# Another order of two stages of a two-block network on one core, and a gating multiply on GpSimd

## The chip, the cores and the metric

The kernel runs on one core of a Trainium2 chip, in float32 with split weights. The metric is the device time of one execution in microseconds (us). Before the change it is 1389.76 us, the median of 3 runs (1389.14 to 1390.28).

## The reference, cut to what matters

One sequence of 256 tokens, width 1024, goes through two layers and then a second block. Each layer is FFN, mixer, FFN. The mixer of layer 0 is causal attention (8 heads of 128, RoPE, normed q and k), that of layer 1 is a Mamba-2 mixer. What the change touches:

```python
# attention: o = softmax(q k^T) v per head, then
x = x + o @ w_o
# Mamba-2: 2048 inner channels, 8 groups of 4 heads of 64, state 128
proj = h @ w_in                      # z (2048), x B C (4096), dt (32)
xbc = silu(causal_conv4(xbc) + conv_b)
y = ssd_chunked(xs * dt, dt * a, B, C)   # two chunks of 128 tokens
y = (y + d_skip * xs) * silu(z)      # the gate
y = y * rsqrt(mean(y * y over each group of 256 channels) + eps) * norm_g
x = x + y @ w_out
```

## The kernel before

**Weights.** Every weight comes as a unit of 512 KB (4 k-tiles of 128 rows by 512 columns) into one of three slots of `raw`. ScalarE (ACT) copies it to `w_hi` in a reduced format (`split_hi`, L374 to L382), VectorE (DVE) subtracts to get `w_lo` (`split_lo`, L384 to L390), and TensorE (PE) multiplies three times, hi by hi, lo by hi, hi by lo. A unit's 24 matmuls of 512 columns set the pace. `split_hi` of unit n waits until PE has used unit n-3, the load of unit n until `w_lo` of unit n-3 is made. SyncE issues the loads.

**Order.** Each engine has one queue, in the order in which its function issues; semaphores join them. Nothing reorders at run time: whatever stands behind a waiting instruction waits too.

**Attention** (`attn_pe` L994, `attn_act` L1068, `attn_dve` L1152). Heads are worked off in slots (`head_slot_*`): in slot s head s is transposed, head s-1 gets its scores, head s-2 its probabilities transposed, head s-3 its output. From slot 5 on, PE fills in tiles of w_o from the table `fill`: `wo_tile(j, k)` is 6 matmuls of unit j with head k, and waits for `oT` of that head, which DVE makes (`prob_dve`, L1224) from ACT's `oT_hi`. In DVE's slot the bias (`bias_dve`, from the scores) comes first, then `oT_lo`, then the probabilities. Two splits of w_o, its units 2 and 3, are issued between slots: unit 2 ahead of slot 4's ACT work, unit 3 after slot 7's.

**Mamba stage** (`ssm_pe` L1283, `ssm_act` L1420, `ssm_pool` L1559, `ssm_dve` L1608). The x, B, C columns come in 8 chunks of 512 channels, channels on partitions: PE multiplies, ACT scales the first tap, DVE adds three taps per tile (12 steps a chunk, L1674), ACT applies Silu. PE turns the x chunks to rows (`ssm_turn`), and the B chunks too, into `b_rows`, which nothing reads. Then comes a loop over the 8 groups, j = 0 to 7, with two items (token chunks) each. PE: one unit of z (`z_unit`, two make a quarter of z), then `scores(2j)`, `scores(2j+1)`, then `outputs(2j-2)`, `outputs(2j-1)`. DVE: `differences` of the running sums, a `split_lo`, `finish` (adds the skip term, gives y), `weigh` (decay times scores). ACT: a copy of a quarter of z every other round (`copy_z` after the change), a split, `exps`, `cross_exps`, `silu_z`, and for a quarter of y `group_squares` and `group_scale`. GpSimd (POOL): `xdt` and `x_skip` of each item, `group_rstd`, and by DMA the running sums of two groups at a time into `cum_early` or `cum_late` (`load_cum`). DVE multiplies y by its gate (`gate_y`, L1714), a quarter at a time. PE then turns the scaled quarters (`turn_y`, L1381), ACT and DVE split them to `yT_hi` and `yT_lo`, and 8 units of w_out follow in the order `OUT_UNITS`: (column half h, quarter q) = (0,0), (0,1), (1,0), (1,1), (0,2), (0,3), (1,2), (1,3). All of the first four need the first two quarters.

Of the kernel before, what the change touches and what calls it, by code (L numbers as in the profile page):

```python
# [24 lines left out]
P = 128  # L25
SEQ = 256
# [118 lines left out]
def build(nc, w, out):  # L145
    with ExitStack() as ctx:
# [135 lines left out]
        b_rows = r("b_rows", [P, GROUPS, P])  # L282
# [711 lines left out]
        def attn_pe(pe):  # L994
            norm_pe(pe, 1, True)
            u = FIRST_UNIT["qkv"]
            for c in range(6):
                if c >= 2:
                    pe.wait_ge(sem("qkv_copied"), TT * (c - 1))
                for j in range(2):  # L1000
                    linear_unit(pe, u + 2 * c + j, 4 * j, KD, hT_hi, hT_lo, pair_banks(c),
                                ("hT", KD * 1) if c == 0 else None)
                    head_slot_pe(pe, 2 * c + j - FIRST_SLOT)
            pe.wait_ge(sem("qkv_copied"), TT * 6)
            u = FIRST_UNIT["wo"]

            def wo_tile(j, k):

                n = BY_ROWS[j][1]
                hi, lo = use_unit(pe, u + j)  # L1010
                pe.wait_ge(sem("oT"), k + 1)
                for t in range(TT):
                    to = psum[:, pair_banks(n)[t], :]
                    a, b = (o[:, k % 4, t * P:(t + 1) * P] for o in (oT_hi[k // 4], oT_lo[k // 4]))
                    pe.matmul(to, a, hi[:, k % 4, :], start=k == 0, stop=False)
                    pe.matmul(to, a, lo[:, k % 4, :], start=False, stop=False)
                    m = pe.matmul(to, b, hi[:, k % 4, :], start=False, stop=k == HEADS - 1)
                if k % 4 == 3:
                    m.then_inc(sem("unit_used"), 1)


            fill = {5: ((0, 0), (0, 1)), 6: ((1, 0), (0, 2)), 7: ((1, 1), (0, 3)), 8: ((1, 2), (1, 3)),
                    9: ((2, 4), (2, 5)), 10: ((2, 6), (3, 4)), 11: ((3, 5), (2, 7), (3, 6), (3, 7))}
# [44 lines left out]
        def attn_act(act):  # L1068
# [3 lines left out]
            for i in range(12):  # L1072
# [15 lines left out]
                split_hi(act, u + i + SLOTS)  # L1088
# [4 lines left out]
                head_slot_act(act, i - FIRST_SLOT)  # L1093
            u = FIRST_UNIT["wo"]
            for slot in range(12 - FIRST_SLOT, HEAD_SLOTS):
                head_slot_act(act, slot)
                if slot == 7:
                    split_hi(act, u + SLOTS)
# [53 lines left out]
        def attn_dve(dve):  # L1152
            u = FIRST_UNIT["qkv"]
            norm_dve(dve, 1, ("mix_norm", 0), True, second_and_third("qkv"))
            for i in range(12):
# [4 lines left out]
                split_lo(dve, u + i + SLOTS)  # L1160
# [3 lines left out]
                if i % 2 == 0 and 1 <= c <= ROPED:  # L1164
                    rope_dve(dve, c - 1)
            u = FIRST_UNIT["wo"]
            for slot in range(12 - FIRST_SLOT, HEAD_SLOTS):
                bias_dve(dve, slot)
                prob_dve(dve, slot)
                if slot == 7:  # L1170
# [96 lines left out]
        OUT_UNITS = [(h, 2 * pair + q) for pair in range(2) for h in range(2) for q in range(2)]  # L1267
# [15 lines left out]
        def ssm_pe(pe):  # L1283
# [22 lines left out]
            for c in range(CHUNKS):  # L1306
# [7 lines left out]
                if 1 <= c <= X_CHUNKS + B_CHUNKS:  # L1314
# [30 lines left out]
            def scores(i):  # L1345
# [4 lines left out]
                else:  # L1350
                    pe.wait_ge(sem("rows"), X_CHUNKS + B_CHUNKS)
# [32 lines left out]
            for j in range(ITEMS // 2 + 1):  # L1384
                if j < ITEMS // 2:
                    z_unit(j)
                    if j == 0:
                        pe.wait_ge(sem("a_sum"), 2)
                        pe.wait_ge(sem("head_rows"), 2)
                if j < ITEMS // 2:  # L1390
                    scores(2 * j)
                    scores(2 * j + 1)
                else:
                    turn_y(0)
# [3 lines left out]
            turn_y(1)  # L1398
            pe.wait_ge(sem("z"), 4)
            for i, (h, q) in enumerate(OUT_UNITS):  # L1400
                if i == 2:
                    pe.wait_ge(sem("y"), ITEMS)
                linear_unit(pe, FIRST_UNIT["ssm_out"] + i, 4 * q, KI, yT_hi, yT_lo, OUT_BANKS[h], ("yT", 0))
                if i in (1, 2):
                    turn_y(i + 1)

        def ssm_turn(pe, c):
# [4 lines left out]
            for i in range(4):  # L1412
                if c < X_CHUNKS:
                    for t in range(TT):
                        m = pe.transpose(psum[:, 4 + t, i * P:(i + 1) * P], xT[:, c % 2, i, t * P:(t + 1) * P], ident)
                else:
                    m = pe.transpose(psum[:, 4, i * P:(i + 1) * P], bcT[:, 4 * (c - X_CHUNKS) + i, 0:P], ident)
            m.then_inc(sem("rows_ready"), 1)

        def ssm_act(act):  # L1420
            norm_act(act, 4, ("mix_norm", KD), False, FIRST_UNIT["ssm_xbc"] - 1 + SLOTS)

            def copy_rows(c):
                act.wait_ge(sem("rows_ready"), c + 1)
                if c < X_CHUNKS:
                    act.activation(xs[:, :, 512 * c:512 * (c + 1)], psum[:, 4:6, :], ACT.Copy).then_inc(sem("rows"), 1)
                else:
                    g = 4 * (c - X_CHUNKS)
                    act.activation(b_rows[:, g:g + 4, :], psum[:, 4, :].rearrange("p (g n) -> p g n", g=4), ACT.Copy)\
                       .then_inc(sem("rows"), 1)  # L1430
# [13 lines left out]
            for c in range(CHUNKS):  # L1444
# [9 lines left out]
                split_hi(act, u + SLOTS)  # L1454
                if c == DT_CHUNK:
# [16 lines left out]
                split_hi(act, u + 1 + SLOTS)  # L1472
                if 1 <= c <= X_CHUNKS + B_CHUNKS:
                    copy_rows(c - 1)
                if c == CHUNKS - 1:
                    exps(0)
                    exps(1)
                    cross_exps(1)
                for i in range(4):
                    tile = 4 * c + i  # L1480
                    act.wait_ge(sem("conv_out"), tile + 1)
# [5 lines left out]
                if c == CHUNKS - 2:  # L1487
                    act.wait_ge(sem("a_sum"), 2)
                    cross_exps(0)
            def group_squares(q):  # L1490

                act.wait_ge(sem("y_gated"), q + 1)
# [25 lines left out]
            for j in range(ITEMS // 2 + 1):  # L1518
                q = j // 2
                if j < ITEMS // 2 and j % 2:  # L1520
                    act.wait_ge(sem("unit_used"), FIRST_UNIT["ssm_z"] + j + 1)
                    act.activation(z[:, :, 512 * q:512 * (q + 1)], psum[:, 0:TT, :], ACT.Copy).then_inc(sem("z"), 1)
                if j < ITEMS // 2:
                    split_hi(act, FIRST_UNIT["ssm_z"] + j + SLOTS)
                if j == ITEMS // 2:
                    act.wait_ge(sem("x_skip"), ITEMS)
                    turned_y(0)
                if 0 < j < ITEMS // 2:
                    exps(2 * j)
                    exps(2 * j + 1)  # L1530
                    if j < ITEMS // 2 - 1:
                        cross_exps(j + 1)
                if j in (3, 7):
                    silu_z(q - 1)
                    silu_z(q)
                if j in (5, 6):
                    group_squares(j - 5)
                if j == 7:
                    group_scale(0)
                    group_scale(1)  # L1540
            u = FIRST_UNIT["ssm_out"] + SLOTS
            turned_y(1)
# [16 lines left out]
        def ssm_pool(pool):  # L1559
# [23 lines left out]
            for i in range(ITEMS):  # L1583
# [16 lines left out]
                if i in (11, 13):  # L1600
                    group_rstd((i - 11) // 2)
# [6 lines left out]
        def ssm_dve(dve):  # L1608
# [5 lines left out]
            def differences(i):  # L1614
# [4 lines left out]
                for hh in range(HPG):  # L1619
# [3 lines left out]
                                             ALU.subtract, ALU.add).then_inc(sem("ssm_diff"), 1)  # L1623

            for c in range(CHUNKS):
# [40 lines left out]
                for j in range(2):  # L1666
                    dve.wait_ge(sem("conv_first"), 4 * c + 2 * j + 2)
# [12 lines left out]
                split_lo(dve, u + 1 + SLOTS)  # L1680

            def weigh(i):
                g, t = divmod(i, TT)
                dve.wait_ge(sem("decay"), i + 1)
                dve.wait_ge(sem("ssm_scores"), i + 1)
                over_heads = lambda scores: scores.unsqueeze(1).broadcast_to([P, HPG, P])
                dve.tensor_tensor(cum(i), cum(i), over_heads(psum[:, 4 + t, 0:P]), ALU.mult).then_inc(sem("within"), 1)
                if t == 0:
                    dve.wait_ge(sem("crossed"), HPG * (g + 1))
                    to = cross[:, g % 2, :, :]  # L1690
                    dve.tensor_tensor(to, to, over_heads(psum[:, 4, P:SEQ]), ALU.mult).then_inc(sem("within"), 1)
# [24 lines left out]
            for j in range(ITEMS // 2 + 1):  # L1716
                if 0 < j < ITEMS // 2:
                    differences(2 * j)
                    differences(2 * j + 1)
                    if j < ITEMS // 2 - 1:  # L1720
                        split_lo(dve, FIRST_UNIT["ssm_z"] + j + SLOTS)
                if j:
                    finish(2 * j - 2)
                    if j == ITEMS // 2:
                        dve.wait_ge(sem("ssm_out"), ITEMS)
                        lo_of_y(0)
                    finish(2 * j - 1)
                if j < ITEMS // 2:
                    weigh(2 * j)
                    weigh(2 * j + 1)  # L1730
                    if j == 0:
                        split_lo(dve, FIRST_UNIT["ssm_z"] + SLOTS)
                else:
                    split_lo(dve, FIRST_UNIT["ssm_z"] + j - 1 + SLOTS)
                if j in (4, 5):
                    gate_y(j - 4)
# [718 lines left out]
```

## Time and profile before

| | |
|---|---|
| median of 3 runs | 1389.76 us |
| profiled execution | 1387.17 us, its span 1385.4 us |
| PE busy | 1355.8 us, 98% of the span |
| DVE, ACT, POOL busy | 881.4, 710.5, 302.2 us |
| attention: heads and w_o | about 242 to 309 us of the span |
| Mamba stage: chunks; loop over groups; output | 707 to 791; 791 to 869; 869 to 915 us |

Busy time is the union of an engine's instructions. A row of the timeline gives start, length, engine, line, what it writes from what, the count of merged instructions, and in brackets how long the engine had stood and what released it.

### The profile page before, as it was taken

How to read it: one execution, taken by the hardware profiler on the slowest of the kernel's cores; microseconds unless marked ns; L12 is line 12 of the kernel's file. 1: busy time of each engine (PE TensorE's matmuls, PEld its weight loads, DVE VectorE, ACT ScalarE, POOL GpSimd, SP SyncE). 2: the span in 40 equal slices, each digit the busy share in tenths (PEclk: the TensorE clock that was granted, in tenths of full speed). 3: DMA queues.
4: the chain of work that ended last, by engine and by line, in shares of the span. 5: the costliest groups of instructions: out<-in, count | busy, mean ns of one | idle time of the engine just before them, and what ended most of it. 6: DMA issues, size and time to landing. Idle time of an engine off the chain costs nothing.

```text
span 1385.4 us, 19574 instructions
## 1 busy us (share of the span) xinstructions
PE 1355.8 (98%) x7607; PEld 1146.6 (83%) x7607; DVE 881.4 (64%) x912; ACT 710.5 (51%) x840; POOL 302.2 (22%) x230
## 2 busy tenths in 40 slices
PE   8999999999999999999999998999999999999997
PEld 7888888778888888888899976888888899888885
DVE  5445568746445565445578798566877556877576
ACT  6444455645444454444557678644434455557543
POOL 3300001000000000000000133029996001535740
PEclk9999999999999999999999999999999999999999
DMA  9555546526555555555454564489675544645341
GB/s 293 195 194 185 182 154 205 167 68 204 191 195 183 182 181 185 182 184 197 134 187 135 203 219 146 132 284 360 233 264 187 168 153 154 209 155 163 117 161 46
DMA packets 158286, 254.09 MB, mean 183 GB/s; under 512 B 8785, under 2 KB 99233, under 8 KB 156561
## 3 DMA queue, kind: packets, MB, share of 16 engines
q1 hardware_dynamic: 155136, 232.94, 51.3%
q0 software_dynamic: 2576, 18.45, 3.6%
q10 hardware_dynamic: 512, 1.85, 0.4%
q8 instruction: 43, 0.70, 0.2%
q14 instruction: 19, 0.15, 0.0%
HBM read 252.12 MB, written 1.08 MB: 183 GB/s over the span
## 4 chain that ended last, share of the span: by engine, by line
PE 81%; issue 8%; DVE 5%; ACT 3%; DMA 2%; SPq 0%; POOL 0%; ACTq 0%; POOLq 0%; DVEq 0%
PE psum L608 11%; PE psum L610 11%; PE psum L609 10%; PE psum L643 5%; PE psum L645 5%; PE psum L644 5%; PE psum L1796 4%; PE psum L1798 3%; PE psum L1797 3%; PE psum L428 3%; PE psum L430 3%; PE psum L429 3%; DVE w_lo L390 3%; ACT w_hi L382 2%; DMA raw<-in_ffn_w_up 1%
## 5 line engine op out<-in xcount | busy, mean ns | idle before, releaser
L390 DVE TENSOR_TENSOR w_lo<-raw,w_hi 128x2048 fp32r<-128x2048 f32 x220 | 548.7, 2498 | 334.0 <-ACT w_hi L382 333.6
L382 ACT ACTIVATE w_hi<-raw 128x2048 fp32r<-128x2048 f32 x220 | 421.3, 1916 | 347.6 <-PE psum L610 124.3
L608 PE MATMUL psum<-w_hi,hT_hi 128*128 128x512 f32 x704 | 278.7, 396 | 2.7 <-DVE w_lo L390 2.1
L610 PE MATMUL psum<-w_hi,hT_lo 128*128 128x512 f32 x704 | 274.7, 390 | 0.0
L609 PE MATMUL psum<-w_lo,hT_hi 128*128 128x512 f32 x704 | 274.3, 390 | 0.0
L608 PEld LDWEIGHTS psum<-w_hi,hT_hi 128*128 128x128 f32 x704 | 132.3, 188 | 31.0 <-DVE w_lo L390 3.3
L610 PEld LDWEIGHTS psum<-w_hi,hT_lo 128*128 128x128 f32 x704 | 132.2, 188 | 28.2
L609 PEld LDWEIGHTS psum<-w_lo,hT_hi 128*128 128x128 f32 x704 | 132.4, 188 | 26.3
L506 POOL TENSOR_TENSOR meansq<-sumsq 128x2 f32<-128x2 f32 x7 | 1.4, 193 | 689.8 <-ACT xn L474 689.8
L643 PE MATMUL psum<-w_hi,hidT_hi 128*128 128x512 f32 x320 | 125.1, 391 | 0.2 <-DVE hid L722 0.2
L645 PE MATMUL psum<-w_hi,hidT_lo 128*128 128x512 f32 x320 | 124.7, 390 | 0.0
L644 PE MATMUL psum<-w_lo,hidT_hi 128*128 128x512 f32 x320 | 124.6, 389 | 0.0
L684 ACT ACTIVATE silu_g<-psum,rstd 128x256 f32<-128x256 f32 x88 | 36.9, 471 | 149.4 <-PE psum L610 149.4
L449 PE MATMUL psum<-hT_hi,w_hi 128*128 128x256 f32 x384 | 109.5, 285 | 0.2 <-DVE hT_lo L500 0.2
L451 PE MATMUL psum<-hT_hi,w_lo 128*128 128x256 f32 x384 | 108.7, 283 | 0.0
L450 PE MATMUL psum<-hT_lo,w_hi 128*128 128x256 f32 x384 | 108.7, 283 | 0.0
L1796 PE MATMUL psum<-w_hi,hT_hi 128*128 128x512 f32 x224 | 88.8, 397 | 0.0
L1798 PE MATMUL psum<-w_hi,hT_lo 128*128 128x512 f32 x224 | 87.3, 390 | 0.0
L1797 PE MATMUL psum<-w_lo,hT_hi 128*128 128x512 f32 x224 | 87.3, 390 | 0.0
L722 DVE SCALAR_TENSOR_TENSOR hid<-psum,rstd,silu_g 128x256 f32<-128x256 f32 x88 | 38.5, 479 | 64.7 <-ACT silu_g L684 64.7
L449 PEld LDWEIGHTS psum<-hT_hi,w_hi 128*128 128x128 f32 x384 | 73.8, 192 | 1.0 <-issue 0.9
L450 PEld LDWEIGHTS psum<-hT_lo,w_hi 128*128 128x128 f32 x384 | 73.8, 192 | 0.0
(378 smaller groups left out, 2157.9 us busy)
## 6 DMA issues: line engine op xcount, KB each, us to landing
raw<-in_ffn_w_down SPq DMA_DIRECT2D x88, 512.0 KB, 4.2
raw<-in_ffn_w_gate SPq DMA_DIRECT2D x87, 512.0 KB, 4.0
raw<-in_ffn_w_up SPq DMA_DIRECT2D x87, 512.0 KB, 5.0
raw<-in_w_in SPq DMA_DIRECT2D x72, 512.0 KB, 4.6
raw<-in_ssm_w_in SPq DMA_DIRECT2D x48, 512.0 KB, 4.6
raw<-in_attn_w_qkv SPq DMA_DIRECT2D x24, 512.0 KB, 4.7
ada_in<-in_w_ada POOLq DMA_DIRECT2D x8, 1536.0 KB, 8.6
raw<-in_ssm_w_out SPq DMA_DIRECT2D x16, 512.0 KB, 4.3
```

Of the source, the lines that this page charges most:

```text
L382: act.activation(w_hi[:, slot, :], raw[:, slot, :], ACT.Copy).then_inc(sem("hi_ready"), 1)
L390: dve.tensor_tensor(w_lo[:, slot, :], raw[:, slot, :], w_hi[:, slot, :].bitcast(F32), ALU.subtract)\
L449: pe.matmul(to, a, hT_hi[:, k, :], start=k == 0 and c % 2 == 0, stop=False, skip_group_check=True)
L450: pe.matmul(to, a, hT_lo[:, k, :], start=False, stop=False, skip_group_check=True)
L608: pe.matmul(to, a, hi[:, kk, :], start=k == 0, stop=False)
L609: pe.matmul(to, a, lo[:, kk, :], start=False, stop=False)
L610: m = pe.matmul(to, b, hi[:, kk, :], start=False, stop=k == KD - 1)
L643: pe.matmul(to, a, hi[:, k, cs], start=begin, stop=False)
L644: pe.matmul(to, a, lo[:, k, cs], start=False, stop=False)
L645: m = pe.matmul(to, b, hi[:, k, cs], start=False, stop=False)
L1796: pe.matmul(to, a, hi[:, kk, :], start=k == 0, stop=False)
L1797: pe.matmul(to, a, lo[:, kk, :], start=False, stop=False)
```

## The change

It moves instructions in the queues, takes the B turns out, and puts two multiplies on another engine. Arithmetic and results are as before.

- Attention: the split of w_o's unit 2 follows slot 4's head work on ACT and DVE; that of unit 3 follows slot 8 on ACT and slot 9 on DVE; tile (3, 4) moves from slot 10 to slot 11.
- `b_rows`, the transposes of the B chunks and their two copies are gone.
- Last chunk (c = 7): on DVE its second split and `weigh(0)`, `weigh(1)` stand between the two halves of the convolution; on ACT `exps(0)`, `exps(1)` come before the second split, `cross_exps(0)` after the first, and the split of z unit 3 before the last two Silu tiles.
- Loop: on ACT the copy of z opens a round and the split closes it; `group_squares`, `group_scale` of quarter 0 move to j = 4 and 5, `silu_z(2)`, `silu_z(3)` behind the loop. `turn_y(0)`, `turned_y(0)` and `lo_of_y(0)` move into j = 6. On PE the last two outputs and `turn_y(1)` follow the first output unit.
- `OUT_UNITS` begins with quarter 0 for both halves.
- POOL multiplies y by its gate for quarters 0 and 1, in items 7 and 10.

```diff
-            fill = {..., 10: ((2, 6), (3, 4)), 11: ((3, 5), (2, 7), (3, 6), (3, 7))}
+            fill = {..., 10: ((2, 6),), 11: ((3, 4), (3, 5), (2, 7), (3, 6), (3, 7))}
...
-        OUT_UNITS = [(h, 2 * pair + q) for pair in range(2) for h in range(2) for q in range(2)]
+        OUT_UNITS = [(0, 0), (1, 0), (0, 1), (1, 1), (0, 2), (0, 3), (1, 2), (1, 3)]
...  ssm_pe
-            for j in range(ITEMS // 2 + 1):
...
+            for j in range(ITEMS // 2):
+                z_unit(j)
...
+                scores(2 * j)
+                scores(2 * j + 1)
                 if j:
                     outputs(2 * j - 2)
                     outputs(2 * j - 1)
-            turn_y(1)
+                if j == 6:
+                    turn_y(0)
             pe.wait_ge(sem("z"), 4)
             for i, (h, q) in enumerate(OUT_UNITS):
+                linear_unit(pe, FIRST_UNIT["ssm_out"] + i, 4 * q, KI, yT_hi, yT_lo, OUT_BANKS[h], ("yT", 0))
+                if i == 0:
+                    outputs(ITEMS - 2)
+                    outputs(ITEMS - 1)
+                    turn_y(1)
                     pe.wait_ge(sem("y"), ITEMS)
+                if i in (2, 3):
+                    turn_y(i)
...  ssm_act
+            copy_z(0)
+            for j in range(1, ITEMS // 2):
+                if j in (3, 5, 7):
+                    copy_z(j // 2)
+                if j == 7:
+                    group_squares(1)
+                exps(2 * j)
+                exps(2 * j + 1)
+                if j < 7:
+                    cross_exps(j + 1)
+                if j == 6:
+                    act.wait_ge(sem("x_skip"), ITEMS // 2 - 1)
                     turned_y(0)
+                split_hi(act, FIRST_UNIT["ssm_z"] + j + SLOTS)
+                if j == 3:
+                    silu_z(0)
+                    silu_z(1)
+                if j == 4:
+                    group_squares(0)
+                if j == 5:
                     group_scale(0)
+            group_scale(1)
+            silu_z(2)
+            silu_z(3)
...  ssm_pool
-                if i in (11, 13):
-                    group_rstd((i - 11) // 2)
+                if i in (7, 10):
+                    q = (i - 7) // 3
+                    cs = slice(512 * q, 512 * (q + 1))
+                    pool.wait_ge(sem("y"), 4 * (q + 1))
+                    pool.wait_ge(sem("z_silu"), q + 1)
+                    pool.tensor_tensor(y[:, :, cs], y[:, :, cs], z[:, :, cs], ALU.mult).then_inc(sem("y_gated_early"), 1)
+                if i in (9, 13):
+                    group_rstd((i - 9) // 4)
...  ssm_dve, last chunk, second half of the taps
+                    if c == CHUNKS - 1 and j:
+                        split_lo(dve, u + 1 + SLOTS)
+                        weigh(0)
+                        weigh(1)
...  ssm_dve, loop
+            for j in range(1, ITEMS // 2):
+                differences(2 * j)
+                differences(2 * j + 1)
+                split_lo(dve, FIRST_UNIT["ssm_z"] + j - 1 + SLOTS)
+                finish(2 * j - 2)
+                finish(2 * j - 1)
+                weigh(2 * j)
+                weigh(2 * j + 1)
+                if j == 6:
+                    lo_of_y(0)
+            split_lo(dve, FIRST_UNIT["ssm_z"] + ITEMS // 2 - 1 + SLOTS)
+            finish(ITEMS - 2)
+            finish(ITEMS - 1)
             gate_y(2)
```

## Rows read from the trace of the kernel before

**Rows 1.** The page, busy time of each engine (share of the span) and instructions.
```profile
PE 1355.8 (98%) x7607; PEld 1146.6 (83%) x7607; DVE 881.4 (64%) x912; ACT 710.5 (51%) x840; POOL 302.2 (22%) x230
```
**Rows 2.** Waits of PE: total us, times, longest.
```profile
PE psum L1381 <- ACT y L1504: 6.3, 1, 6.3
...
PE psum L1015 <- DVE hT_lo L1224: 2.4, 2, 1.7
```
**Rows 3.** Windows: us, busy (instructions) of PE, PEld, DVE, ACT, POOL; granted clock; DMA; GB/s.
```profile
803.10:810.00 6.90, 3.89 (x53) 3.33 (x53) 6.90 (x10) 5.97 (x6) 0.59 (x1) 0.79 0.70 239
810.00:858.00 48.00, 48.00 (x456) 39.78 (x456) 45.26 (x91) 35.64 (x65) 23.91 (x30) 1.00 0.59 207
```
**Rows 4.** Timeline of PE, attention: start, us, engine, line, operation, count, idle before.
```profile
274.93 0.77 PE L1015 MATMUL psum<-w_hi,oT_hi 128*128 128x512 f32 x1 [2.46 <-DVE oT_lo L1224]
...
277.63 0.55 PE L1036 MATMUL psum<-qkT 128*128 128x128 f32 x2
...
279.78 0.48 PE L1015 MATMUL psum<-w_hi,oT_hi 128*128 128x512 f32 x1
...
282.61 0.39 PE L1036 MATMUL psum<-qkT 128*128 128x128 f32 x2
...
297.13 0.47 PE L1015 MATMUL psum<-w_hi,hT_hi 128*128 128x512 f32 x1 [1.70 <-DVE hT_lo L1224]
```
**Rows 5.** Timeline of DVE, attention.
```profile
272.16 2.29 DVE L390 TENSOR_TENSOR w_lo<-raw,w_hi 128x2048 fp32r<-128x2048 f32 x1 [1.16 <-ACT w_hi L382]
...
293.17 2.29 DVE L390 TENSOR_TENSOR w_lo<-raw,w_hi 128x2048 fp32r<-128x2048 f32 x1 [1.05 <-ACT w_hi L382]
```
**Rows 6.** Timeline of PE, start of the loop over groups.
```profile
806.11 1.12 PE L1353 MATMUL psum<-bcT 128*128 128x256 f32 x4 [3.07 <-DVE cross L1691]
807.15 1.13 PE L1367 MATMUL psum<-xdt,cum_early 128*64 128x64 f32 x16
...
809.91 0.74 PE L1340 MATMUL psum<-w_hi,hT_hi 128*128 128x512 f32 x1
...
816.49 0.69 PE L1367 MATMUL psum<-xdt,cum_early 128*64 128x64 f32 x16
...
818.04 0.50 PE L1340 MATMUL psum<-w_hi,hT_hi 128*128 128x512 f32 x1
```
**Rows 7.** Timeline of PE, end of that loop and output stage.
```profile
864.29 1.97 PE L1381 MATMUL psum<-const,y 128*128 128x128 f32 x8 [6.26 <-ACT y L1504]
866.19 1.12 PE L1367 MATMUL psum<-xdt,cum_late 128*64 128x64 f32 x16
...
868.76 1.09 PE L1381 MATMUL psum<-const,y 128*128 128x128 f32 x8
...
880.61 1.04 PE L1381 MATMUL psum<-const,y 128*128 128x128 f32 x8
```
**Rows 8.** Timeline of PE, one of two groups of B transposes.
```profile
766.05 0.60 PE L1417 MATMUL psum<-const,bcT 128*128 128x128 f32 x4
```
**Rows 9.** Timeline of DVE, convolution of the last chunk.
```profile
797.39 5.27 DVE L1674 SCALAR_TENSOR_TENSOR conv<-psum,taps,conv 128x255 f32<-128x255 f32 x12
```
**Rows 10.** Timeline of ACT, end of the loop.
```profile
844.62 1.28 ACT L1441 ACTIVATE cross<-cum_late,rest 128x128 f32<-128x128 f32 x4 [0.93 <-DMA cum_late<-cum_rows]
...
856.39 1.90 ACT L382 ACTIVATE w_hi<-raw 128x2048 fp32r<-128x2048 f32 x1
...
862.55 3.28 ACT L1504 ACTIVATE y<-y,y_rstd 128x256 f32<-128x256 f32 x8
```
**Rows 11.** Timeline of POOL in the loop.
```profile
810.09 3.54 POOL L1591 TENSOR_TENSOR xdt<-xs,dt 128x256 f32<-128x256 f32 x1 [5.99 <-PE psum L1367]
...
837.67 0.59 POOL L1567 DMA_DIRECT2D cum_late<-cum_rows  x1
```
**Rows 12.** Two lines of code: duration in ns, min/median/max, first and last start, forms.
```profile
L836 POOL TENSOR_TENSOR ada<-ada,ada_term x21: 2389/2414/4483, 940.4 to 1051.0; 128x1024 f32<-128x1024 f32 x21
...
L390 DVE TENSOR_TENSOR w_lo<-raw,w_hi x220: 2264/2293/8972, 14.1 to 1363.9; 128x2048 fp32r<-128x2048 f32 x110
```

More of the change, by code:

```diff
@@ L1096, in attn_act @@
                 head_slot_act(act, slot)
-                if slot == 7:
+                if slot == 8:
                     split_hi(act, u + SLOTS)
@@ L1165, in attn_dve @@
                     rope_dve(dve, c - 1)
+            split_lo(dve, u + 11 + SLOTS)
             u = FIRST_UNIT["wo"]
@@ L1169, in attn_dve @@
                 prob_dve(dve, slot)
-                if slot == 7:
+                if slot == 9:
                     split_lo(dve, u + SLOTS)
@@ L1382, in turn_y @@
                     m.then_inc(sem("y_turned"), 1)
-            for j in range(ITEMS // 2 + 1):
[L1385 to L1394, printed above, removed]
+            for j in range(ITEMS // 2):
+                z_unit(j)
+                if j == 0:
+                    pe.wait_ge(sem("a_sum"), 2)
+                    pe.wait_ge(sem("head_rows"), 2)
+                scores(2 * j)
+                scores(2 * j + 1)
                 if j:
@@ L1412, in ssm_turn @@
             for i in range(4):
[L1413 to L1417, printed above, removed]
+                for t in range(TT):
+                    m = pe.transpose(psum[:, 4 + t, i * P:(i + 1) * P], xT[:, c % 2, i, t * P:(t + 1) * P], ident)
             m.then_inc(sem("rows_ready"), 1)
@@ L1424, in copy_rows, with copy_z @@
                 act.wait_ge(sem("rows_ready"), c + 1)
[L1425 to L1430, printed above, removed]
+                act.activation(xs[:, :, 512 * c:512 * (c + 1)], psum[:, 4:6, :], ACT.Copy).then_inc(sem("rows"), 1)
+            def copy_z(q):
+                act.wait_ge(sem("unit_used"), FIRST_UNIT["ssm_z"] + 2 * q + 2)
+                act.activation(z[:, :, 512 * q:512 * (q + 1)], psum[:, 0:TT, :], ACT.Copy).then_inc(sem("z"), 1)
             def exps(i):
@@ L1454, in ssm_act @@
                 split_hi(act, u + SLOTS)
+                if c == CHUNKS - 1:
+                    act.wait_ge(sem("a_sum"), 2)
+                    cross_exps(0)
                 if c == DT_CHUNK:
@@ L1480, in ssm_act @@
                     tile = 4 * c + i
+                    if tile == 4 * CHUNKS - 2:
+                        split_hi(act, FIRST_UNIT["ssm_z"] + SLOTS)
                     act.wait_ge(sem("conv_out"), tile + 1)
@@ L1516, in turned_y @@
                        .then_inc(sem("yT_hi"), 1)
[L1518 to L1526, printed above, removed]
-                    turned_y(0)
[L1528 to L1538, printed above, removed]
+            copy_z(0)
[10 more added lines that the diff above has]
+                    act.wait_ge(sem("x_skip"), ITEMS // 2 - 1)
+                    turned_y(0)
+                split_hi(act, FIRST_UNIT["ssm_z"] + j + SLOTS)
[5 more added lines that the diff above has]
+                if j == 5:
                     group_scale(0)
-                    group_scale(1)
+            group_scale(1)
+            silu_z(2)
+            silu_z(3)
             u = FIRST_UNIT["ssm_out"] + SLOTS
+            act.wait_ge(sem("x_skip"), ITEMS)
             turned_y(1)
@@ L1623, in differences, with weigh @@
                                              ALU.subtract, ALU.add).then_inc(sem("ssm_diff"), 1)
+            def weigh(i):
+                g, t = divmod(i, TT)
+                dve.wait_ge(sem("decay"), i + 1)
+                dve.wait_ge(sem("ssm_scores"), i + 1)
+                over_heads = lambda scores: scores.unsqueeze(1).broadcast_to([P, HPG, P])
+                dve.tensor_tensor(cum(i), cum(i), over_heads(psum[:, 4 + t, 0:P]), ALU.mult).then_inc(sem("within"), 1)
+                if t == 0:
+                    dve.wait_ge(sem("crossed"), HPG * (g + 1))
+                    to = cross[:, g % 2, :, :]
+                    dve.tensor_tensor(to, to, over_heads(psum[:, 4, P:SEQ]), ALU.mult).then_inc(sem("within"), 1)
             for c in range(CHUNKS):
@@ L1679, in ssm_dve @@
                                 step.then_inc(sem("conv_out"), 1)
[L1680 to L1691, printed above, removed]
+                if c < CHUNKS - 1:
+                    split_lo(dve, u + 1 + SLOTS)
             y_order = in_order(dve, "vector_order")
```

54 lines of the change are left out of this document (16 added, 38 removed).

## The prediction

> **What bounds the kernel now.** I read the page's busy shares first: TensorE is busy 1355.8 of 1385.4 us [rows 1], so only two things can move the time: matmuls that disappear, and stretches in which PE stands. Next the waits of PE, longest first [rows 2]: 6.3 us in one piece for the transposes of y (L1381), and among the small ones L1015 in the attention. Then the granted clock by windows [rows 3]: 0.79 of full in 803 to 810 us against 1.00 in 810 to 858. At its two levels, 2.4 and 1.2 GHz, PE ran at the lower for part of the first window, right after it had stood. So a stall costs its length and then slow matmuls. Last the timelines around each stall, PE first, then the queue that releases it.
>
> **The change part by part.** The engines run in order, so each part is a queue that is reordered; what counts is which instruction PE then meets last.
>
> *Attention.* PE stands 2.46 us before tile (0,1) of w_o at 274.93, and its 6 matmuls then last 2.70 us to 277.63 [rows 4], where two tiles at full clock take 282.61 - 279.78 = 2.83, one 1.41 [rows 4]. Lost: 2.46 + 1.29 = 3.75. The releaser, oT_lo, stood behind a 2.29 us w_lo split on DVE that starts at 272.16 [rows 5]. The change puts that split, and its w_hi half on ACT, behind the head's work. It does not vanish: w_hi now starts after the exponentials, and w_lo sits in front of the bias of slot 5 and of the next oT_lo. A head slot's scores would come at 273.7, the split would hold DVE to about 276.8, three bias steps and oT_lo take some 1.6, and PE, done with (1,0) at about 277.3, goes on at 278.6. I charge 1.2 us (bounds 0 and 2.5), at full clock: after the 1.70 us wait at 295 to 297 the matmul at 297.13 lasts 0.47 [rows 4], against 0.77 after the 2.46 one. Gain 2.5. The second split, at 293.17 [rows 5], delayed bias and oT_lo of slot 8, for 1.70 of the 2.4 us in [rows 2]. It goes behind slot 9, and its only reader, tile (3,4), moves one slot later; there it would be ready within 0.2 us of need. Gain 1.7, cover: tile (2,6) and one head. The last 0.7 us of that row stays (bounds 0 and 0.7). Attention: **4.2 us** (bounds 1.7 and 6.2).
>
> *B transposes.* The turns of the B chunks (L1417) and their copies to b_rows, read nowhere, go: two groups of 4, 0.60 us busy each [rows 8], of which some 0.15 lies under the next matmul. PE works through there without a wait, so 2 x 0.45 = **0.9 us** (bounds 0 and 1.2).
>
> *First Mamba stall.* scores(2) at 806.11 waits 3.07 us for DVE's weigh(0), which stands behind the whole convolution of the last chunk (12 steps, 5.27 us from 797.39 [rows 9]) and a split. Then, at the low clock, the outputs last 809.91 - 807.15 = 2.76 against 818.04 - 816.49 = 1.55, and the next unit's first matmul 0.74 against 0.50 [rows 6]. Lost: 3.07 + 1.21 + 0.24 = 4.52, the two pairs of slow score matmuls between not counted. Now weigh(0) and weigh(1) stand between the halves of that convolution. Their inputs are there: the exponentials move ahead of ACT's split, and scores(0), (1) come after z unit 0, at 796.7. DVE has half the convolution and a split before it, so weigh ends near 800, and PE asks at 802.9. The late half of the convolution then ends at 802.6, where it did before, so its Silu tiles and the broadcast load behind them do not move. Next is copy_z(0), which overwrites no bank before 804 and which PE needs at 805.2. Gain **4.5** (bounds 3 and 4.5).
>
> *Second Mamba stall.* turn_y(0) at 864.29 waits 6.26 us for ACT, which is in group_scale (8 pieces, 3.28 us from 862.55 [rows 10]) behind exponentials, a table load and two silu_z. Then the 8 transposes last 1.97 against 1.04 at full clock, and outputs 868.76 - 866.19 = 2.57 against 1.55 [rows 7, 6]. Lost: 6.26 + 0.93 + 1.02 = 8.21. Now quarter 0 is scaled in j = 5 and turned by PE in j = 6; units (0,0) and (1,0) need only that quarter, and give 11 us of cover to the last outputs, the other silu_z and quarter 1. What is late next is the turn in j = 6: it wants group_scale(0), which ACT reaches after cross_exps(6), which needs the second load into cum_late. Before, that load was issued at 837.67 and used at 844.62, 6.95 us later [rows 11, 10]. POOL can now issue it at about 833, since it has the first multiply (2.4 us, below) in front but no longer waits for a late finish. Then used at 840, plus 1.28 cross, 1.90 split [rows 10] and 4 of the 8 scale pieces, 1.64: ready at 844.8, and PE asks for it at 844.4. I charge 0.5 us (bounds 0 and 4, where a clock loss would be added). Gain **7.7** (bounds 3.5 and 8.2).
>
> *The multiply on GpSimd.* On DVE it cost PE nothing: in 810 to 858 PE is busy 48.00 of 48 us, DVE 45.26 with both multiplies in it [rows 3]. So taking them off frees no PE time; it gives DVE room for lo_of_y(0), which moves there. What it adds: a POOL tensor_tensor of this shape lasts 2.41 us (median of L836), 4.48 at most [rows 12]. x_dt and x_skip stand behind it. The second one would start at 838.9 and x_dt(11) be ready near 842, for outputs at 843.6. When DVE reads two SBUF operands at the same time, one of them stops: x_dt took 3.54 us at 810.09 under a w_lo split, and that split, 2.29 as a median, reaches 8.97 in the stretch where POOL computes ada [rows 11, 12]. I charge 0.2 us (bounds 0 and 5), nearest to the median row, since two short multiplies are no dense stretch.
>
> The Trainium skill, *SBUF — State Buffer*, section *Who interferes with whom*, has the rule for this: a VectorE instruction with two SBUF inputs and a GpSimd instruction that reads SBUF exclude each other for a whole instruction, and the one that starts first wins. By that rule each multiply holds DVE at most once, and the charge would be 0 to 2 x 2.4; the 8.97 row, where POOL issues back to back, is longer than one POOL instruction, so the rule alone undercounts it. The Trainium skill, *GPSIMD Engine Reference*, *Engine selection*, advises against such a multiply on GpSimd.
>
> **Sum.** 4.2 + 0.9 + 4.5 + 7.7 - 0.2 = 17.1 us. The profiled execution took 1387.17 us (span 1385.4 and 1.8 around it), so it would take 1370.1. The median of the runs is 1389.76, 2.6 above the profiled one; on it I predict 1372.7. Bounds of all terms together: 1.7 + 0 + 3 + 3.5 - 5 = 3.2 at the least, 6.2 + 1.2 + 4.5 + 8.2 = 20.1 at the most: 1386.6 and 1369.7.
>
> **Rivals.**
> *A, a new wait in place of each old one.* PE stands at turn_y(0) in j = 6 (the load and scale chain 3 us later than I walked), and the oT wait returns at slot 6. For it: the margins in my walk are below 1 us at three places, and PE follows its queue in order, so z unit 7 waits too. Against: the chain is 6 us earlier than it was. Price: 3 - 0.5 = 2.5 more, 1.9 for slow matmuls as after the old stall, 2.5 in the attention: gain 10.2, **1379.6**.
> *B, all stalls close,* also the 0.7 us in the attention. For it: my charges of 1.2 and 0.5 rest on differences of a few tenths between queues. Against: a queue that loses a tenth anywhere keeps a wait. Gain 17.1 + 1.2 + 0.7 + 0.5 - 0.2 = 19.3, **1370.5**.
> *C, slower: GpSimd becomes the bound.* Place: rounds j = 4 and 5, where POOL has four elementwise pieces, the multiply, and the rstd in one round. If each piece is stretched as at 810.09, 4 x 3.54 = 14.2, and the multiply to 4.48, a round takes 18.6 against PE's 8.1 (818.04 - 809.91 [rows 6]). That is 10.5 late in each of two rounds, 21.0 in all, and 1389.76 - 17.3 + 21.0 = **1393.5**. It decides against the change from 17.3 us of such delay, nearly all of both rounds. Against: the pieces take 0.6 us unless a split runs over them, and there is one split per round. By the rule of the Trainium skill named above, too, a piece can only be held by one DVE instruction at a time.
> *D, the change does not do what it says.* The order on PE would leave the last outputs or the transposes waiting as long as before, only later, under the output units: gain 4.2 + 0.9 + 4.5 = 9.6, **1380.2**. Against: quarter 1 has a whole unit of 5.5 us and more of cover.
>
> **How the numbers follow.** Forecast 0.56, B 0.15, A 0.13, D 0.06, C 0.04, and 0.06 for A with more places wrong than it counts (1384 to 1392). "Same" means within 0.2%, 2.8 us of 1389.76, about what a measurement of this kernel can tell from no change. Faster: 0.56 + 0.15 + 0.13 + 0.06 and half of the last 0.06, 0.93; same 0.02, slower 0.05, both from C and the last. The range runs from 2 us under B, where every term is at its upper bound and the runs' own spread of 1.1 us is added, to just under A: 1368.5 to 1379. It leaves out C, the last case, D's centre and about half of A, 0.18 to 0.2.
>
> **What would show it.** Right: no wait of PE above 2 us in the attention or the Mamba stage; L1417 gone; scores(2) right behind z unit 1; a granted clock of 1.00 from 790 to 900; POOL's multiplies near 2.4 us; output stage ending about 13 us earlier, the attention about 4. Wrong: a wait of L1381 on L1504 in j = 6 above 1.5 us (A); L1367 waiting for x_dt (C); a wait of L428 for yT (D); an oT wait above 2 us in slot 6, with the slow matmuls behind it.

## The result and the profile after

The changed kernel takes 1369.14 us in the median of 4 runs (1368.81 to 1371.25); the kernel before took 1389.45 us beside it (1387.7 to 1390.28, 4 runs). The ratio is 0.9865 (95% interval 0.9853 to 0.9877). The prediction was 1372.7 us, between 1368.5 and 1379: the time lies inside, 3.6 us under the forecast. The profiled execution took 1369.46 us, span 1367.7, against 1387.17 and 1385.4. Of the kernels below, one execution of e8 is left out of its median: 1498.71 us, at a mean granted clock of 0.848 where its others have 0.995 to 0.997.

The page, busy time of each engine, beside [rows 1]:

```profile
PE 1349.9 (99%) x7599; PEld 1143.5 (84%) x7599; DVE 879.1 (64%) x910; ACT 709.1 (52%) x838; POOL 311.6 (23%) x232
```

TensorE does the same work but for 8 transposes and is busy 5.9 us less: 1.2 of it are those transposes (two groups of 0.60 [rows 8]), the rest is mostly matmuls that no longer run at the low clock. The other 11.8 of the 17.7 us of span were standing time. Waits of PE (total us, times, longest), beside [rows 2]:

```profile
PE psum L607 <- DVE w_lo L389: 2.2, 3, 1.3
...
PE psum L1014 <- DVE oT_lo L1227: 1.3, 1, 1.3
PE psum L1014 <- DVE hT_lo L1227: 0.7, 1, 0.7
PE psum L1343 <- issue: 0.6, 1, 0.6
```

The 6.3 us wait for the transposes is gone, and the whole Mamba loop has one wait left. Windows of the attention and of the loop with the output units, beside [rows 3] (busy time and instructions of PE, PEld, DVE, ACT, POOL; granted clock; DMA share; GB/s):

```profile
240.00:305.00 65.00, 63.01 (x323) 53.33 (x322) 45.68 (x85) 38.39 (x72) 1.65 (x2) 1.00 0.40 132
786.00:900.00 114.00, 113.15 (x853) 94.94 (x853) 94.61 (x160) 86.52 (x157) 40.00 (x41) 1.00 0.57 193
```

Timeline of PE: the wait that the moved split leaves in slot 6, the one that stays in slot 10, the first outputs, the wait before z unit 6, and the three turns of y, beside [rows 4, 6, 7]:

```profile
278.57 0.47 PE L1014 MATMUL psum<-w_hi,oT_hi 128*128 128x512 f32 x1 [1.29 <-DVE oT_lo L1227]
...
295.89 0.47 PE L1014 MATMUL psum<-w_hi,hT_hi 128*128 128x512 f32 x1 [0.70 <-DVE hT_lo L1227]
...
797.93 0.69 PE L1370 MATMUL psum<-xdt,cum_early 128*64 128x64 f32 x16
...
831.59 0.47 PE L1343 MATMUL psum<-w_hi,hT_hi 128*128 128x512 f32 x1 [0.58 <-issue]
...
839.44 1.09 PE L1384 MATMUL psum<-const,y 128*128 128x128 f32 x8
...
855.36 1.09 PE L1384 MATMUL psum<-const,y 128*128 128x128 f32 x8
...
867.36 1.04 PE L1384 MATMUL psum<-const,y 128*128 128x128 f32 x8
```

In these two stages no matmul behind a wait is slow now, 0.47 us against 0.77 at 274.93 [rows 4]. Timeline of DVE and of POOL where the new multiplies stand:

```profile
274.60 2.29 DVE L389 TENSOR_TENSOR w_lo<-raw,w_hi 128x2048 fp32r<-128x2048 f32 x1 [1.05 <-ACT w_hi L381]
...
834.65 5.02 DVE L1635 SCALAR_TENSOR_TENSOR cum_late<-cum_late,a_sum,const 128x128 f32<-128x128 f32 x8
```
```profile
822.74 2.61 POOL L1613 TENSOR_TENSOR y<-y,z 128x1024 f32<-128x1024 f32 x1 [4.22 <-ACT z L1516]
...
826.44 0.59 POOL L1575 DMA_DIRECT2D cum_late<-cum_rows  x1
...
834.59 2.39 POOL L1613 TENSOR_TENSOR y<-y,z 128x1024 f32<-128x1024 f32 x1
```

### The profile page after: what moved, and what is told of

Same layout as the page of the kernel before. It is cut to its first block, busy times and chain, and to the rows that moved or that the text cites. A ratio compares the mean times of both kernels' runs of the same rounds, so it can differ in the third digit from the quotient of the medians.

```text
span 1367.7 us, 19554 instructions
## 1 busy us (share of the span) xinstructions
PE 1349.9 (99%) x7599; PEld 1143.5 (84%) x7599; DVE 879.1 (64%) x910; ACT 709.1 (52%) x838; POOL 311.6 (23%) x232
## 4 chain that ended last, share of the span: by engine, by line
PE 93%; DVE 3%; ACT 1%; issue 1%; DMA 1%; SPq 0%; POOL 0%; POOLq 0%; DVEq 0%; ACTq 0%
PE psum L607 11%; PE psum L609 11%; PE psum L608 11%; PE psum L644 5%; PE psum L642 5%; PE psum L643 5%; PE psum L1807 4%; PE psum L1808 3%; PE psum L1809 3%; PE psum L448 3%; PE psum L449 3%; PE psum L450 3%; PE psum L427 3%; PE psum L429 3%; PE psum L428 3%; DVE w_lo L389 2%
```

## The experiments

Three places of the profiled execution measure where time went, since a span alone scatters by 1 to 2 us (last section): the start of z unit 0, the start of the 16 transposes (L538, L539 before) that follow the output units ("loop end"), and the span. These places scatter too: in the kernels that have the changed attention and no B turns, z unit 0 starts between 785.54 and 786.08 us, so differences of half a us at one place are no finding. The kernel before ran beside each group of kernels; its median was 1387.7 us beside e1 to e4, 1388.4 beside e5 to e10 and 1389.5 beside the changed kernel and e11. So compare medians within a group, and ratios across groups.

| kernel | median us | ratio to before (95%) | z unit 0 | loop end | span |
|---|---|---|---|---|---|
| before | 1389.45 | 1 | 791.29 | 915.03 | 1385.4 |
| changed | 1369.14 | 0.9865 (0.9853 to 0.9877) | 785.60 | 896.34 | 1367.7 |
| e1 attention only | 1383.01 | 0.9970 (0.9960 to 0.9981) | 786.63 | 911.01 | 1382.9 |
| e2 gates on VectorE | 1369.02 | 0.9868 (0.9853 to 0.9882) | 786.08 | 897.48 | 1367.5 |
| e3 weighing late | 1368.38 | 0.9860 (0.9845 to 0.9874) | 785.98 | 896.07 | 1367.8 |
| e4 old output order | 1372.91 | 0.9899 (0.9885 to 0.9913) | 785.66 | 897.85 | 1367.7 |
| e5 B turns back | 1369.62 | 0.9866 (0.9851 to 0.9882) | 786.66 | 897.72 | 1367.6 |
| e6, 1 more multiply | 1372.20 | 0.9877 (0.9860 to 0.9894) | 785.77 | 901.00 | 1372.2 |
| e6, 3 more | 1383.86 | 0.9963 (0.9951 to 0.9976) | 785.79 | 911.18 | 1382.3 |
| e7 turn behind the loop | 1376.38 | 0.9915 (0.9901 to 0.9929) | 785.98 | 903.08 | 1374.3 |
| e8 cross early | 1376.32 | 0.9912 (0.9894 to 0.9930) | 785.54 | 903.23 | 1374.5 |
| e9 cross early, weighing late | 1374.41 | 0.9904 (0.9888 to 0.9919) | 786.05 | 901.75 | 1371.5 |
| e10 two moves | 1368.29 | 0.9853 (0.9839 to 0.9867) | 784.14 | 896.68 | 1366.5 |
| e11 three moves | 1369.23 | 0.9859 (0.9843 to 0.9875) | 784.23 | 895.84 | 1366.8 |

**e1.** The kernel before with the changed `fill` and the four moved splits of the attention, nothing else.

> The kernel before with the attention edits alone. Theory (stalls of PE close, and what is moved costs 1.2 us in slot 6): 4.7 us faster than before, as the first matmul of ffn2_0 came 4.74 us earlier in the changed kernel (311.97 to 307.23). Rival (the attention gain is swallowed by the loads that follow, and shows only together with the Mamba edits): less than 1 us faster, ffn2_0 waiting for w_lo.

The median is 4.7 us lower (1383.01 beside 1387.70), as expected. z unit 0 starts 4.66 us earlier, 5.69 in the changed kernel. So the attention is worth 4.7 and the rest of that stretch, the B transposes, 1.0, give or take the scatter of the place.

**e2.** The multiplies of quarters 0 and 1 go back to VectorE:

```diff
-                if i in (7, 10): ... pool.tensor_tensor(y[:, :, cs], y[:, :, cs], z[:, :, cs], ALU.mult)
+                if j in (4, 5):
+                    gate_y(j - 4)
```

> The changed kernel with the gates of quarters 0 and 1 back on VectorE, at the end of rounds 4 and 5. Theory (the multiply was hidden on either engine; the order of the queues is the whole gain): within 1.5 us of the changed kernel, about 18 to 20 us faster than before. Rival (moving the multiply to GpSimd made room that VectorE needs): PE waits for weigh or turn_y(0), 3 us or more slower than the changed kernel. Rival (the multiply on GpSimd costs, by shutting out VectorE): 1 us or more faster than the changed kernel.

Same time. Which engine multiplies is worth nothing that can be measured; the gain is in the reordering. In the profiled execution the loop end is 1.14 us later. Of this 0.48 is there at z unit 0, and TensorE waits 0.81 us longer before z unit 6 (1.39 us in place of 0.58), behind sums whose load GpSimd issued at 811.73 in place of 810.32, ahead of either multiply.

**e3.** `weigh(0)`, `weigh(1)` go behind the whole convolution of the last chunk.

> The changed kernel with weigh(0) and weigh(1) behind the whole last convolution again. Theory: the first Mamba stall comes back, but shorter than 3.07 us, since the split is no longer between: weigh would end near 799.3 of the changed trace instead of 795, the scores are asked at 797.2, so 1 to 2.5 us of wait and 0 to 1.5 for a lower clock behind it; 1.5 to 4 us slower than the changed kernel. Rival (another queue held PE there): no change.

A miss: no stall came back. Timelines of DVE and of PE, the end of `weigh(0)` and the third scores:

```profile
796.68 0.68 DVE L1648 TENSOR_TENSOR cross<-cross,psum 128x512 f32<-128x512 f32 x1
```
```profile
797.57 0.93 PE L1356 MATMUL psum<-bcT 128*128 128x256 f32 x4
```

VectorE is done at 797.4 us, and TensorE, which asks at 797.6, does not wait. The margin is 0.2 us; in the changed kernel it is 2.7 (794.4 and 797.2). So the place of the weighing, which the prediction held for the cure, gives room and is not the cure. e8 and e9 look for the real one.

**e8 and e9.** The first cross exponentials back to where they stood, e9 with e3's edit too:

```diff
                 split_hi(act, u + SLOTS)
-                if c == CHUNKS - 1:
-                    act.wait_ge(sem("a_sum"), 2)
-                    cross_exps(0)
 ...
+                if c == CHUNKS - 2:
+                    act.wait_ge(sem("a_sum"), 2)
+                    cross_exps(0)
```

> The changed kernel with the first cross exponentials, which need the load of the sums, put back on ScalarE to the end of the chunk before, ahead of the last chunk's split; weighing stays between the halves of the convolution. Theory now: what made VectorE late for the first scores was that ScalarE waited 2.3 us for that load and VectorE 5.1 us for the split behind it. Then most of the stall returns here: 2 to 4 us slower than the changed kernel (1371 to 1373 us) if weighing's place does not help, under 1 us if either of the two edits alone is enough.

> As the one before, and weighing behind the whole convolution too, so that both edits of the first stall are undone. Expected: the wait before the third scores is back, 3 us and its slow matmuls, 4 to 5 us slower than the changed kernel (1373 to 1374 us). If it is within 1 us of the changed kernel, the stall was closed by something else, the exponentials ahead of the second split or the late z split.

They lose 6.9 (e8) and 5.4 us (e9) at the loop end, more than the 2 to 4 and 4 to 5 expected. What they bring back can be seen in the kernel before, timelines of ACT and DVE:

```profile
788.66 1.28 ACT L1441 ACT_TABLE_LOAD   x1 [2.32 <-DMA cum_early<-cum_rows]
```
```profile
793.07 2.29 DVE L390 TENSOR_TENSOR w_lo<-raw,w_hi 128x2048 fp32r<-128x2048 f32 x1 [5.09 <-ACT w_hi L382]
```

Timelines of ACT and DVE of e9:

```profile
784.10 1.28 ACT L1440 ACT_TABLE_LOAD   x1 [2.11 <-DMA cum_early<-cum_rows]
785.40 1.28 ACT L1440 ACTIVATE cross<-cum_early,rest 128x128 f32<-128x128 f32 x4
786.58 1.90 ACT L381 ACTIVATE w_hi<-raw 128x2048 fp32r<-128x2048 f32 x1
```
```profile
788.52 2.29 DVE L389 TENSOR_TENSOR w_lo<-raw,w_hi 128x2048 fp32r<-128x2048 f32 x1 [4.87 <-ACT w_hi L381]
```

and of ACT and DVE of the changed kernel:

```profile
781.44 1.90 ACT L381 ACTIVATE w_hi<-raw 128x2048 fp32r<-128x2048 f32 x1
784.05 1.28 ACT L1440 ACT_TABLE_LOAD   x1 [0.71 <-DMA cum_early<-cum_rows]
```
```profile
780.90 4.85 DVE L389 TENSOR_TENSOR w_lo<-raw,w_hi 128x2048 fp32r<-128x2048 f32 x2
```

The load lands at 784.1 in both. Ahead of the split, the exponentials make ScalarE stand for it, then take 2.5 us, and only then comes the split that VectorE waits 4.87 us for: VectorE's queue is late by that, and TensorE stands 3.75 us for `weigh`, at a granted clock of 0.83 in 800 to 810 us. In e8 the load landed 2.4 us later (786.5), and TensorE waited 2.4 us for `weigh` and 4.5 more before three z units: weighing between the halves did not keep the time from being lost. So the cure is the split ahead of the exponentials that need a transfer: without it the stall is back wherever the weighing stands. That this move alone would have closed the stall in the kernel before was not run.

**e5.** The B transposes and their copies to `b_rows` back.

> The changed kernel with the 16 transposes of the B chunks and their two copies to b_rows put back. Expected: 0.9 us slower than the changed kernel (start of the z units 0.9 us later), that is about 1370 us, at the edge of what the medians can tell; the trace decides by the start of z unit 0, at 785.6 us in the changed kernel. The rival: the turns also delay something else (ScalarE's copies in front of the Silu tiles), and more than 1.5 us comes back.

z unit 0 is 1.06 us later than in the changed kernel, and later than in any kernel without the B turns, as in e1; the medians can't tell it (ratio 0.9866 against 0.9865). The wait before z unit 6 is 1.06 us here in place of 0.58.

**e4.** `OUT_UNITS` begins (0, 0), (0, 1) again.

> The changed kernel with the old order of the first output units, (0,0), (0,1), (1,0). Theory: unit 1 then needs quarter 1, whose last yT_lo ended at 858.9 of the changed trace while PE asked at 856.3: a wait of about 2.7 us on yT_lo and slow matmuls behind it for up to 1.5, 2.5 to 4.5 us slower than the changed kernel. Rival (the order of units is immaterial, the transposes alone were late): no change.

The wait is there, for the low half of quarter 1 (timeline of PE):

```profile
857.85 0.47 PE L427 MATMUL psum<-w_hi,yT_hi 128*128 128x512 f32 x1 [1.51 <-DVE yT_lo L1717]
```

It costs 1.5 us at the loop end of the profiled execution, shorter than the 2.7 expected and with no slow matmul behind it. That execution (1369.48) is the fastest of four; the median is 3.9 us above that of e2 and 4.5 above that of e3, in the same group. What the other three lost is not shown. The low clock can't be all of it: one took 1373.44 us at a mean granted clock of 0.999, the same as in the profiled one.

**e7.** `turn_y(0)`, its copies and its low halves go behind the loop, all else as changed.

> The changed kernel with the turn of quarter 0 of y (transposes, their copies to yT_hi, the low halves) moved behind the loop over the z units, as it stood before, but with quarter 0 scaled early as in the change. If early scaling alone closes the second stall, TensorE waits only for the copies and low halves of the turned quarter, 2 to 4 us, since unit (0,0) follows the turn at once: 1371 to 1373 us. If it is the place of the turn, the 6.3 us wait and its slow matmuls return, 1377 us.

The wait was in the expected range and the cost twice as high. Timeline of PE, the first, the third and the thirteenth matmul of unit (0, 0):

```profile
852.63 0.77 PE L427 MATMUL psum<-w_hi,yT_hi 128*128 128x512 f32 x1 [3.65 <-DVE yT_lo L1714]
...
853.62 0.63 PE L429 MATMUL psum<-w_hi,yT_lo 128*128 128x512 f32 x1
...
857.86 0.39 PE L427 MATMUL psum<-w_hi,yT_hi 128*128 128x512 f32 x1
```

The first 12 matmuls run at the low clock and take 857.86 - 852.63 = 5.23 us; the next 12, at full clock, take 2.75. So 3.65 + 2.5 = 6.1 of the 6.7 us that the loop end moves; 0.4 more is there at z unit 0. My expectation left the clock out. Of the 8.3 us that the second stall gave, turning quarter 0 inside the loop is 6.4, counted from z unit 0; scaling it early and the new order of the units are worth 1.9 without it.

**e6.** One or three more multiplies of the same shape on GpSimd, into a scratch tile, behind each of the two:

```diff
+                    for _ in range(k):
+                        order(pool.tensor_tensor(scratch, x[:, :, 0:512], x[:, :, 512:1024], ALU.mult))
```

> The changed kernel with one more GpSimd multiply of the same shape (128 x 1024, inputs from SBUF, result into a scratch tile) behind each of its two gating multiplies. If GpSimd has the slack that its row of the profile suggests, the first one is free and only the second makes x_dt(11) late: 1 to 2 us slower than the changed kernel, 1369 to 1372 us. If GpSimd were near to being the bound (rival C), both cost their 2.4 us and the clock after them: 5 us and more slower.

> The changed kernel with three more such multiplies behind each of the two gating ones, 7.2 us each time. This should be beyond the slack, so that TensorE waits for x_dt behind them: some 4 us each time, with slow matmuls after the wait, 6 to 12 us slower than the changed kernel (1375 to 1382 us). If the time stays within 2 us, GpSimd has a whole round of slack and rival C was far off.

Timelines of PE, one more multiply and then three:

```profile
831.54 0.34 PE L1371 MATMUL psum<-xdt,cross 128*64 128x64 f32 x4 [1.22 <-issue]
841.55 0.34 PE L1371 MATMUL psum<-xdt,cross 128*64 128x64 f32 x4 [1.81 <-issue]
```
```profile
833.63 1.12 PE L1371 MATMUL psum<-xdt,cum_early 128*64 128x64 f32 x16 [3.97 <-issue]
...
851.11 0.48 PE L1371 MATMUL psum<-xdt,cross 128*64 128x64 f32 x4 [5.95 <-issue]
```

With 2.4 us more TensorE waits 1.2 and 1.8 us. The expectation that the first one is free was wrong, though the gating multiply ahead of it also began 1.2 us later there (823.94 against 822.74). The slack is read from the changed kernel itself: x_dt(9) is ready at 827.68 and wanted at 829.9, x_dt(11) at 837.60 and wanted at 838.4, so 2.2 and 0.8 us. The profiled execution (1374.03) is the slowest of its four; its loop end moves by 4.7 us, 3.0 of it waits. The other 1.7 are mostly slow matmuls behind the second wait: the turn of y takes 1.65 us in place of 1.09 and the next six matmuls start 0.4 to 0.6 us apart in place of 0.2 to 0.3. By the ratio the kernel is 1.7 us slower, inside the 1 to 2 expected. With 7.2 us more the loop end moves by 14.8, above the 6 to 12 expected, 10.7 of it waits, the rest mostly clock (0.91 in 810 to 850 us). GpSimd is a bound close by, but the change stays inside it.

**e10 and e11.** Two tries to beat the changed kernel. In both the w_o split on VectorE moves into slot 5:

```diff
                 dve.tensor_tensor(to, psum[:, 7, 0:SEQ], hi.bitcast(F32), ALU.subtract).then_inc(sem("oT"), 1)
+            if slot == 12 - FIRST_SLOT:
+                split_lo(dve, FIRST_UNIT["qkv"] + 11 + SLOTS)
```

e10: `copy_z(2)` ahead of `group_squares(0)`, the second GpSimd multiply at item 11. e11: `copy_z(2)` ahead of the split of j = 4, VectorE's last split behind `gate_y(2)`, the multiply at item 10.

> The changed kernel with two waits taken away: in the attention the w_o split on VectorE goes into the head slot after, between oT_lo and the reciprocal, where VectorE waits 1.5 us for the exponentials anyway (closes the 1.29 us wait of TensorE at 278.57), and on ScalarE the copy of z quarter 2 goes ahead of the squares of quarter 0 (closes the 0.58 us wait at 831.59), with GpSimd's second multiply one item later. Expected: 1.5 to 1.9 us faster than the changed kernel, 1367.3 to 1367.7 us. The rival: the split in its new place delays the probabilities of that head and the wait moves to their transposes in the next slot, within 0.5 us of the changed kernel.

> The attention move of the kernel before (the w_o split into the next head slot, worth 1.3 us at the start of the z units) kept, with two others in place of its second: ScalarE copies z quarter 2 ahead of the split of j = 4, not behind it, and VectorE puts its last split behind the finish of the last item and the gating of quarter 2, so that GpSimd's last x_skip does not run under it. Where the two moves left the gain in waits of 0.5, 0.4 and 0.9 us at 830, 854 and 857 us, these should be gone: 1.5 to 2 us faster than the changed kernel in the span, 1366 us, and a median of 1367 to 1367.7 us. The rival: the later split frees its buffer later, or the last quarter's gating comes late, and TensorE waits in the output units instead; then it is no faster than the changed kernel.

The attention move does what it should: the wait at 278.57 is gone, z unit 0 starts 1.4 us earlier in both. But e10 has given it all back at the loop end, most of it in waits (timeline of PE, e10, then e11). The first follows ScalarE's copy of z and the last VectorE's y; the profile does not name what released the second:

```profile
830.23 0.47 PE L1344 MATMUL psum<-w_hi,hT_hi 128*128 128x512 f32 x1 [0.49 <-issue]
853.55 0.34 PE L1371 MATMUL psum<-xdt,cross 128*64 128x64 f32 x4 [0.43 <-issue]
856.65 0.50 PE L427 MATMUL psum<-w_hi,yT_hi 128*128 128x512 f32 x1 [0.93 <-DVE y L1725]
```
```profile
838.01 0.34 PE L1371 MATMUL psum<-xdt,cross 128*64 128x64 f32 x4 [1.43 <-issue]
```

e11 closes those three and meets GpSimd instead: x_dt(11) stands behind the multiply (POOL of e11):

```profile
834.94 2.35 POOL L1616 TENSOR_TENSOR y<-y,z 128x1024 f32<-128x1024 f32 x1
837.25 0.65 POOL L1602 TENSOR_TENSOR xdt<-xs,dt 128x256 f32<-128x256 f32 x1
```

Neither time can be told from the changed kernel's (ratios 0.9853 and 0.9859 against 0.9865), and both were expected 1.5 to 2 us under it. e11 with the multiply at item 11, as in e10, which has no wait there, was not tried.

## Why the prediction was right, step by step

Measured at the places above, the parts sum to 4.7 + 1.0 + 4.7 + 8.3 = 18.7 us, where 17.1 was forecast; 1.0 is lost later, and the span is 17.7 shorter. The executions of the kernel before scatter above its profiled one and those of the changed kernel do not, so the medians differ by more (20.3 us, 18.8 by the ratio).

- **Attention, 4.2 forecast, 4.7 measured (e1).** The walk held to the tenth: split until 276.9 (276.8 walked), TensorE on at 278.57 (278.6), wait 1.29 (1.2 charged), 0.70 stays. Of the 0.5 more, 0.16 is clock: the head's matmuls behind the old wait, which the terms left out, took 2.15 us (277.63 to 279.78), the next slot's 1.99. Another 0.26 lies behind the stage, in the transposes ahead of the next FFN (2.55 us before, 2.29 in e1), at a granted clock of 1.00 in both.
- **B transposes, 0.9 forecast, 1.0 to 1.1 measured** (e1, e5).
- **First stall, 4.5 forecast, 4.7 measured, by a wrong reason.** From z unit 0 to the first outputs it is 12.33 us where it was 15.86, and the matmuls behind are fast. The step "now weigh(0) and weigh(1) stand between the halves" is not what closed it: e3 undoes it and loses nothing. What closed it is `cross_exps(0)` behind the split (e8, e9). The prediction read VectorE's queue back to the convolution and stopped there; two rows ahead, the split at 793.07 that had waited 5.09 us for ScalarE, had the cause. The size came out since the stall is the same whoever ends it, and so that this term is right is luck.
- **Second stall, 7.7 forecast, 8.3 measured.** The early turn, the covered last outputs and the load before the scaling are as forecast. The walk kept the times of the kernel before from z unit 0 on, 5.69 us later than those of the changed kernel: its load at 833 was issued at 826.44 + 5.69 = 832.1, and its turn, wanted at 844.4, starts at 839.44 + 5.69 = 845.1. The 0.5 charged for that turn did not occur, it starts without a wait. A smaller wait that the walk had missed stands in the same round, 0.58 us before z unit 6. It ends with the copy of z (830.49 to 831.49), which ScalarE does behind `group_squares(0)`.
- **GpSimd's multiply, -0.2 forecast, nothing measured (e2).** It takes 2.61 and 2.39 us there, and 1.22 and 1.63 on VectorE in e2.

The lock between the two engines is in the trace: the 8 subtractions of L1635 at 834.65, which began with the second multiply, take 5.02 us, 2.18 elsewhere. VectorE was held 2.8 us, a little longer than one multiply of 2.39. The Trainium skill, *SBUF — State Buffer*, section *Who interferes with whom*, says that two such instructions exclude each other for a whole one; the trace agrees, but for some tenths: two GpSimd pieces of 0.66 us follow the multiply at once. An instruction can also lose to two of the other engine in a row: the x_dt of 3.54 us at 810.09 [rows 11] ran under the last subtractions of VectorE (to 810.95) and then the whole split (810.87 to 813.15), 2.9 us longer than its usual 0.6. The lock at 834.65 cost TensorE nothing, as VectorE had the room.

Of the rivals, A did not occur beyond what was charged; B, all stalls closed, is nearest in time (1370.5) but not in kind, since 1.29 and 0.70 stay. D is refuted: unit (0,0) covers the last outputs (no wait at 853 to 868), and e4 shows its price, 1.5 us and more, if the order is left. C's mechanism is real and was not reached: it shows with 2.4 us more per round, or when TensorE comes 1.8 us earlier (x_dt(11), wanted at 836.6 in e11), and it takes 7.2 to lose most of the gain (e6). Two slips of the prediction change no verdict: B's sum takes the 0.2 off a second time (19.5 us, not 19.3), and tile (3,4) is the first reader of w_o's unit 3, not its only one.

## What to carry to other kernels

Where an in-order queue is late, follow it back past the long instruction to the last time that it stood, and ask what its releaser waited for; here four exponentials that needed a DMA, ahead of a split that needed none, cost 5 to 7 us. Keep what waits for a transfer behind what doesn't. Undo each edit of a bundle by itself before you credit it, and price a wait of TensorE with the slow matmuls that may follow: 2.5 us behind one of 3.65 in e7, 1.7 behind one of 1.81 in e6, and none behind the one of 1.70 in the kernel before [rows 4].

## What was not expected

At the stage behind the loop, 32 matmuls of one column last 3.6 us in the profiles of before, e1 to e5 and e10, and 3.86 to 4.82 in those of the changed kernel, e6 to e9 and e11, with the 16 transposes behind them slow too, 3.4 to 3.7 us (changed kernel, then e10, timelines of PE):

```profile
1087.92 4.72 PE L949 MATMUL psum<-const,ada 128*128 128x1 f32 x32
1092.50 3.65 PE L538 MATMUL psum<-const,xn 128*128 128x128 f32 x16
```
```profile
1088.15 3.63 PE L949 MATMUL psum<-const,ada 128*128 128x1 f32 x32
1091.82 2.00 PE L538 MATMUL psum<-const,xn 128*128 128x128 f32 x16
1095.23 0.35 PE L448 MATMUL psum<-hT_hi,w_hi 128*128 128x256 f32 x1 [1.41 <-DVE hT_lo L2263]
```

Every instruction there is the same in both; the granted clock is 0.66 in 1090 to 1100 us in the one and 1.00 in the other. Slow transposes alone cost nothing: before they take 3.48 us too, and in e10 TensorE waits 1.41 us behind the fast ones. From those matmuls to the end the profiles take 278.3 to 280.5 us (1367.7 - 1087.92 = 279.8 in the changed kernel, 278.6 before), while from the loop end to them all take 191.2 to 191.8. The longest two, e1 and e3 with 280.5, have fast one-column matmuls and a low clock later (0.91 in the stretch from 10 to 20 us behind the start of the 32), so those matmuls are not the only place. No edit of these kernels is near it. So 1.2 us of the gain were lost in the profiled execution, by chance as far as is known, and a span says little of differences under 2 us; a marker inside it does. What decides the clock there stays open.
